# Channel-major products split over the two row halves of the matmul array

## What is computed

```
# first block
u = rmsnorm(x, norm_mix_g)
p = u @ w_in + b_in                                   # 1024 x 7424: q, kv, hq, hf, hi, hg, ga, gb
y_attn = sliding_window_sink_attention(aq, ak, av)    # 16 heads, window 128
y_hgrn = hgrn2_branch(hq, hf, hi, hg)                 # 8 heads, chunks of 64
merged = sigmoid(gate_a) * (y_attn @ w_branch_attn) + sigmoid(gate_b) * (y_hgrn @ w_branch_hgrn)
h = x + merged @ w_out
h = h + (silu(u2 @ w_ffn_gate) * (u2 @ w_ffn_up)) @ w_ffn_down
# second block
z, xbc, dt, q, k, v = split(h2 @ w_in_2)
x = x + g_m * (concat(ssd_mixer(z, xbc, dt), chunk_attention(q, k, v)) @ w_out_2)
x = x + g_f * ((silu(g) * val) @ w_down_2)            # g, val = causal_dwconv(h3 @ w_up_2)
```

## Time and profile before

| | |
|---|---|
| median of three runs | 795.62 us (795.6 to 796.41) |
| profiled execution, first to last instruction (span) | 794.3 us |
| what the median has beyond the span | 1.3 us |
| PE busy | 782.8 us, 99% |
| PE weight loads busy | 713.8 us, 90% |
| DVE busy | 598.9 us, 75% |
| ACT busy | 490.2 us, 62% |
| DMA | 161.1 MB, 203 GB/s on average |
| channel-major matmuls (L1799) | 3288 |

### The profile page before, as it was taken

The page is one execution under the profiler, slowest core; times in us unless marked ns, Lnnn a source line. Parts: engine busy times, 40 slices in busy tenths (PEclk is TensorE's granted clock), DMA queues, the critical chain, the costliest instruction groups (busy, mean ns, idle before and its releaser), DMA issues. The chain is left out here.

```text
span 794.3 us, 13466 instructions
## 1 busy us (share of the span) xinstructions
PE 782.8 (99%) x5534; PEld 713.8 (90%) x5534; DVE 598.9 (75%) x804; ACT 490.2 (62%) x746; POOL 17.9 (2%) x38
## 2 busy tenths in 40 slices
PE   8999999999999999999999999999999999999996
PEld 8999979999999888888888888999789999999885
DVE  5576786667876867787869897897968787777464
ACT  6778889567743565444434267966758767666441
POOL 3000001000200000000000000001000000000000
PEclk9999999999999999999999999999999999999999
DMA  8873544457444467799878993734362756555611
GB/s 303 295 240 134 191 130 158 160 169 256 160 159 160 158 214 257 233 308 310 283 277 299 359 364 122 258 112 157 107 212 87 256 164 206 165 166 180 238 54 54
DMA packets 105677, 161.10 MB, mean 203 GB/s; under 512 B 4480, under 2 KB 51856, under 8 KB 105616
## 3 DMA queue, kind: packets, MB, share of 16 engines
q1 hardware_dynamic: 105472, 159.97, 60.2%
q10 hardware_dynamic: 144, 0.26, 0.1%
HBM read 159.16 MB, written 1.06 MB: 202 GB/s over the span
## 5 line engine op out<-in xcount | busy, mean ns | idle before, releaser
L1127 DVE TENSOR_TENSOR wL<-raw,wH 128x2048 fp32r<-128x2048 f32 (+2 forms) x142 | 284.5, 2008 | 88.1 <-ACT wH L715 83.7
L1799 PE MATMUL ps<-p1H,wH 128*128 128x256 f32 x968 | 276.8, 287 | 1.8 <-DVE arena L1127 0.8
L1799 PE MATMUL ps<-p1H,wL 128*128 128x256 f32 x968 | 273.2, 283 | 0.0
L1799 PE MATMUL ps<-p1L,wH 128*128 128x256 f32 x968 | 271.8, 283 | 0.0
L715 ACT ACTIVATE wH<-raw 128x2048 fp32r<-128x2048 f32 (+1 forms) x114 | 211.9, 1863 | 85.4 <-PE ps L1802 43.6
L1799 PEld LDWEIGHTS ps<-p1H,wH 128*128 128x128 f32 x968 | 185.4, 192 | 6.4 <-issue 2.6
L1799 PEld LDWEIGHTS ps<-p1H,wL 128*128 128x128 f32 x968 | 185.5, 192 | 0.0
L1799 PEld LDWEIGHTS ps<-p1L,wH 128*128 128x128 f32 x968 | 184.8, 192 | 0.1
L1802 PE MATMUL ps<-wH,p1H 128*128 128x512 f32 (+1 forms) x236 | 91.1, 386 | 0.0
L1802 PE MATMUL ps<-wL,p1H 128*128 128x512 f32 (+1 forms) x236 | 90.2, 382 | 0.0
L1802 PE MATMUL ps<-wH,p1L 128*128 128x512 f32 (+1 forms) x236 | 90.1, 382 | 0.0
(11 more groups left out here) (306 smaller groups left out, 1018.4 us busy)
## 6 DMA issues: line engine op xcount, KB each, us to landing
raw<-in_w_in SPq DMA_DIRECT2D x37, 1024.0 KB, 5.1
raw<-in_w_ada SPq DMA_DIRECT2D x24, 1024.0 KB, 5.5
raw<-in_w_up SPq DMA_DIRECT2D x44, 512.0 KB, 4.8
raw<-in_w_ffn_gate SPq DMA_DIRECT2D x22, 512.0 KB, 4.5
raw<-in_w_ffn_up SPq DMA_DIRECT2D x22, 512.0 KB, 5.9
raw<-in_w_ffn_down SPq DMA_DIRECT2D x10, 1024.0 KB, 5.5
raw<-in_w_down SPq DMA_DIRECT2D x10, 1024.0 KB, 5.1
raw<-in_w_out SPq DMA_DIRECT2D x8, 1024.0 KB, 5.1
```

Of the source, the lines that this page charges most:

```text
L1127: return v.tensor_tensor(o, a, b, op)
L1799: last = mm(ps[:, t[1], 0:T], wt[:, slot, k, t[2]:t[2] + P], at_[:, k0 + k, :], start=st, stop=en)
```

## The change

Channel-major panels that came to the last branch of `panel` get one of their own. Each 128-row product is written as two products of 64 rows. A panel goes in four steps: tiles (0, 1), (2, 3), (1, 0), (3, 2). In a step, the first tile of the pair takes its lower 64 rows (partitions 0 to 63) of all four row blocks and the second its upper 64 rows, in turns, upper first; two steps later the halves are changed over, so that each tile has had both. The number of matmuls and of weight loads of such a panel doubles, to 96. Before each step PE waits until the step before the last has ended (`halves_written`), counted on a new semaphore `row_halves` or on `tile_done`. In a last part the tiles 0 and 1 end with the third step, 2 and 3 with the fourth. The operands, the accumulation in the banks and all other branches stay. To have a semaphore to spare, the ten of `hprep` that one engine each raises in a fixed order (on ACT hE1 to hE5, on DVE hdm, hQp, hKp, hdl, hKk) become two counters, `h_exp` and `h_mul`; the waits name the same events.

```diff
+H_EXP = {"mid": 1, "-mid": 2, "start": 3, "chunk": 4, "end": 5}
+H_MUL = {"mid": 1, "q": 2, "k": 3, "end": 4, "k_end": 5}
...
+        def h_exp(s, what):
+
+            return on.h_exp, 5 * s + H_EXP[what]
+
+        def h_mul(s, what):
+
+            return on.h_mul, 5 * s + H_MUL[what]
...
@@ the matmul engine, hA @@
-                    pe.wait_ge(on.hKp, s + 1)
-                    pe.wait_ge(on.hKk, s + 1)
+                    pe.wait_ge(*h_mul(s, "k_end"))
...
@@ the matmul engine, panel @@
+            halves_written, halved = [], [0]
+
             def panel(name, part):
                 q = PIDX[name, part]
                 g = GROUPS[name]
@@ -1850,6 +1855,35 @@
                                 last = product(t, k, only=(1,))
                         if name in NORM_OF and k < 2:
                             late_turn(NORM_OF[name], 6 + k)
+                elif [t[0] for t in g["tiles"]] == ["cm"] * 4:
+                    for step_, (low, high) in enumerate(((0, 1), (2, 3), (1, 0), (3, 2))):
+                        for written in halves_written[-2] if len(halves_written) > 1 else ():
+                            pe.wait_ge(*written)
+                        halves_written.append([])
+                        first_visit = part == 0 and step_ < 2
+                        for m in sorted((low, high)) if first_visit else ():
+                            if (name, m) in BANKFREE:
+                                pe.wait_ge(*BANKFREE[name, m])
+                        for k in range(nk):
+                            if step_ == 0 and name in FIRST_USE:
+                                pe.wait_ge(*operand_ready(name, k0 + k))
+                            for x, (wt, at_) in enumerate(((wH, aH), (wH, aL), (wL, aH))):
+                                for m, rs in ((high, slice(C, P)), (low, slice(0, C))):
+                                    _, bank, c = g["tiles"][m]
+                                    last = mm(ps[:, bank, 0:T], wt[rs, slot, k, c:c + P], at_[rs, k0 + k, :],
+                                              start=first_visit and k == 0 and x == 0,
+                                              stop=final and step_ > 1 and k == nk - 1 and x == 2)
+                                    if final and step_ > 1 and k == nk - 1 and x == 2:
+                                        last.then_inc(on.tile_done, 1)
+                                        halves_written[-1] = [(on.tile_done, TILE[name, m])]
+                                    elif k == nk - 1 and x == 2 and m == 3 and step_ == 3:
+                                        halves_written[-1].append(USED[q])
+                                    elif k == nk - 1 and x == 2:
+                                        last.then_inc(on.row_halves, 1)
+                                        halved[0] += 1
+                                        halves_written[-1] = [(on.row_halves, halved[0])]
+                        if (name, part, step_) == ("bc", 0, 1):
+                            dt_turn()
                 else:
                     for m, t in enumerate(g["tiles"]):
                         if part == 0 and (name, m) in BANKFREE:
```

More of the change, by code:

```diff
@@ L250, in build @@
         on.g_done = ctx.enter_context(nc.semaphore("g_done"))
[L251 to L258, removed]
+        on.h_exp = ctx.enter_context(nc.semaphore("h_exp"))
+        on.h_mul = ctx.enter_context(nc.semaphore("h_mul"))
         on.hQq = ctx.enter_context(nc.semaphore("hQq"))
@@ L264, in build @@
         on.hb_done = ctx.enter_context(nc.semaphore("hb_done"))
-        on.hdl = ctx.enter_context(nc.semaphore("hdl"))
-        on.hdm = ctx.enter_context(nc.semaphore("hdm"))
         on.hf_log = ctx.enter_context(nc.semaphore("hf_log"))
@@ L274, in build @@
         on.hs_done = ctx.enter_context(nc.semaphore("hs_done"))
+        on.row_halves = ctx.enter_context(nc.semaphore("row_halves"))
         on.hsh = ctx.enter_context(nc.semaphore("hsh"))
@@ L675, in _ @@
                 elif e[0] == "hprep" and e[2] == 2:
-                    pool.wait_ge(on.hE3, e[1] + 1)
-                    pool.wait_ge(on.hQp, e[1] + 1)
+                    pool.wait_ge(*h_exp(e[1], "start"))
+                    pool.wait_ge(*h_mul(e[1], "q"))
                     pool.tensor_tensor(hQ, hQ, T2, ALU.mult).then_inc(on.hQq, 1)
@@ L1043, in _ @@
                     if e[2] == 0:
-                        act.wait_ge(on.hdm, s + 1)
-                        nc.scalar.activation(T2, T1, ACT.Exp).then_inc(on.hE1, 1)
+                        act.wait_ge(*h_mul(s, "mid"))
+                        nc.scalar.activation(T2, T1, ACT.Exp).then_inc(on.h_exp, 1)
                     elif e[2] == 1:
-                        act.wait_ge(on.hE1, s + 1)
-                        nc.scalar.activation(T1, T1, ACT.Exp, scale=-1.0).then_inc(on.hE2, 1)
+                        act.wait_ge(*h_exp(s, "mid"))
+                        nc.scalar.activation(T1, T1, ACT.Exp, scale=-1.0).then_inc(on.h_exp, 1)
                     elif e[2] == 2:
-                        act.wait_ge(on.hQp, s + 1)
-                        nc.scalar.activation(T2, hB, ACT.Exp).then_inc(on.hE3, 1)
-                        nc.scalar.activation(E5[:], hB[:, :, C - 1:T:C], ACT.Exp).then_inc(on.hE5, 1)
-                    else:
-                        act.wait_ge(on.hdl, s + 1)
-                        nc.scalar.activation(T1, T1, ACT.Exp).then_inc(on.hE4, 1)
+                        act.wait_ge(*h_mul(s, "q"))
+                        nc.scalar.activation(T2, hB, ACT.Exp).then_inc(on.h_exp, 1)
+                        nc.scalar.activation(E5[:], hB[:, :, C - 1:T:C], ACT.Exp).then_inc(on.h_exp, 1)
+                    else:
+                        act.wait_ge(*h_mul(s, "end"))
+                        nc.scalar.activation(T1, T1, ACT.Exp).then_inc(on.h_exp, 1)
                         if s:
@@ L1558, in _ @@
                         dve.wait_ge(on.hk_done, 4 * s + 4)
-                        tt(f(T1), bc, bc[:, :, C // 2 - 1:C // 2].broadcast_to([P, 16, C]), ALU.subtract).then_inc(on.hdm, 1)
+                        tt(f(T1), bc, bc[:, :, C // 2 - 1:C // 2].broadcast_to([P, 16, C]), ALU.subtract).then_inc(on.h_mul, 1)
                     elif e[2] == 1:
@@ L1562, in _ @@
                             dve.wait_ge(on.scores_done, NU1)
[L1563 to L1566, removed]
+                        dve.wait_ge(*h_exp(s, "mid"))
+                        tt(hQp, hQ, T2, ALU.mult).then_inc(on.h_mul, 1)
+                        dve.wait_ge(*h_exp(s, "-mid"))
+                        tt(hKp, hK, T1, ALU.mult).then_inc(on.h_mul, 1)
                     elif e[2] == 2:
-                        dve.wait_ge(on.hKp, s + 1)
-                        tt(f(T1), bc[:, :, C - 1:C].broadcast_to([P, 16, C]), bc, ALU.subtract).then_inc(on.hdl, 1)
+                        dve.wait_ge(*h_mul(s, "k"))
+                        tt(f(T1), bc[:, :, C - 1:C].broadcast_to([P, 16, C]), bc, ALU.subtract).then_inc(on.h_mul, 1)
                     elif e[2] == 3:
-                        dve.wait_ge(on.hE4, s + 1)
-                        tt(hK, hK, T1, ALU.mult).then_inc(on.hKk, 1)
+                        dve.wait_ge(*h_exp(s, "end"))
+                        tt(hK, hK, T1, ALU.mult).then_inc(on.h_mul, 1)
                 elif k == "hA":
@@ L1583, in _ @@
                     bank = (7, 5, 6)
-                    dve.wait_ge(on.hE5, s + 1)
+                    dve.wait_ge(*h_exp(s, "chunk"))
                     dve.wait_ge(on.hkv_psum, 2 * s + 1)
```

## The result

The changed kernel takes 802.68 us (median of 4 runs, 802.36 to 802.89), the kernel before 795.88 beside it (795.6 to 796.41): a ratio of 1.0082, interval 1.0070 to 1.0093. The forecast was 781.2. The profiled execution spans 800.9 us, against 794.3: 6.6 us more, where 14.4 less were forecast.

What follows compares the result with a forecast made beforehand. PE was taken to bound the kernel; 22.3 us less for products, 5.9 more for changes of form and 2.0 more for tile ends and softmax gave 14.4 less: 781.2 us from 795.6, range 770 to 803 (0.9).

Steps and rivals of the forecast that it cites:

- The products: 2784 channel-major products on PE, each split into a pair of halves: pitch from 0.120 to 0.112 us, 22.3 us less.
- rows 5: Trace rows of hB before the change: 64-row products streaming 128 columns at the slow rate, 0.112 us a pair.
- rows 6: Trace rows before the change: full products that stream 128 columns, 0.110 us apiece.
- Loads of halves cost nothing more: In a pair on PE, the second half with its own weight load adds no time; by the skill's pricing, 259 us.
- Changes of form: PE switching between full rows and 64 rows or other forms: 31 more changes at 0.19 us, 5.9 us more.
- Waits between the halves of a panel: PE's wait before each of a panel's four steps for the step before the last: 0.
- Tiles that end later: Tiles ending in twos in last parts: 0.7 us more at k2, whose scores wait for ACT's copies; 0 elsewhere.
- Softmax beside the panels: Attention stretch, probabilities not ready at pt, units 0 and 1 with little room: 1.3 us more, including similar in hgrn and ssd.
- Semaphores: Ten semaphores merged into two counters, each wait naming the same event: 0.
- The bubble stays with each half: Rival: the 0.013 us gap belongs to every weight change, pair pitch stays 0.120; 802.5 us, chance 0.16.
- Two fast streams don't go together: Rival: a pair of halves costs what 512 columns do, 0.227 us; 1100 us in all, chance 0.08.
- The other two: Rivals: bubble goes altogether, pitch 0.109 to 0.110, 775.5 us, chance 0.13; tiles' ends hold it, 787 us, chance 0.06 (787 to 793).

Runs made afterwards that it cites:

- the last kernels: Kernel before, but both token operands stream past held high weights as one 512-column matmul: in u1 to u10 800.3 us, in six of these groups 794.99 us.
- the kernel of other forms: Changed kernel with u1 to u10 in pairs, single halves, quarters, single quarters or whole products, some matmuls left out; pitch 0.12 us, no comparable total.

## Why the prediction failed, step by step

*The products, 22.3 us less: the step that failed.* It said "I take 0.112, the pitch of the only half-array pairs with the same loads". Measured is 0.120 for 2784 pairs, so 0.0, the lower bound that I had named ("none of it goes, 0.120"). The pairs of rows 5 streamed 128 columns, where a whole product has 0.112 as well (the prediction had this from rows 6); they bounded the load and told nothing of what lies above it. The choice between the bounds went by the row that looked most like the new instructions (rows held, columns loaded), not by the row that shared what was in question (columns streamed at the fast rate, with its gap). The only such rows were the earlier trace rows, 0.120 and 0.227, which show the same 0.013 at both sizes: I had put this under "for it" and weighed it at 0.16.

*Loads of halves cost nothing more:* right. Two loads a pair pass in 0.12 us, and even four a set of quarters. The Trainium skill ("TensorE: Matmul & The Clock Gate", section LDWEIGHTS (loading the stationary operand)) is right of one load, 128 columns at an estimated 107 ns beside the floor of 111, and loads for different rows are not to be added up.

*Changes of form, 5.9 us:* right in kind and nearly in size. 0.19 was read at hB, and 0.177 is the mean of 20 in u. The first panel came 0.41 us earlier and the last 6.55 later. Of these 6.96, 2.3 are the waits at hf0, hi0 and k2; 4.6 remain, 0.15 for each of 31. Three places gave back 0.6 to 0.7 us each, which is part of why it is less than 31 x 0.177 = 5.5; smaller shifts of waits, either way, weren't added up. At z it was PE's wait of 0.7 for DVE in the kernel before (at L2104), which is gone. Behind each of the two hB the next panel's upper halves start while hB's last products, in the lower half alone, still go (timeline of PE, after; L2050 is hB):

```profile
155.57 0.61 PE L2050 MATMUL ps<-arena 64*128 64x128 f32 x4
155.91 0.38 PE L1873 MATMUL ps<-p1H,wH 64*128 64x256 f32 x1
156.01 0.38 PE L2050 MATMUL ps<-arena 64*128 64x128 f32 x2
156.13 0.28 PE L1873 MATMUL ps<-p1L,wH 64*128 64x256 f32 x1
```

From the start of hB to the next panel it is 1.98 us before and 1.35 after; some 0.2 of that are the changes of form that are gone, the rest is work that ran on idle rows. Halves do gain where rows are idle, as here.

*Waits between the halves of a panel, 0:* right, all 20 panels of u are as long as before.

*Tiles that end later:* the sum had 0.7 at k2, and 0.95 came. Elsewhere I wrote 0, with the reason that transposes, scores or `pt` lie between. At hq0 and hf0 that reason was wrong: nothing there waits for a bank, but the softmax of the next unit waits for ACT and DVE, which were held up, 0.86 and 0.53. I priced the last tile, and it was the first one that moved furthest, from a quarter to three quarters of the part.

*Softmax beside the panels, 1.3 us:* some 1.4 was lost, at unit 3, for which I had foreseen room of 0.5 to 1 us, and at unit 4, which I had left out for its token-major panel. At unit 1, where I saw no room, pt costs 0.31, its two changes of form and no wait. A right number with the wrong cause, by luck: it belongs to the tiles' ends.

*Semaphores, 0:* right, 0.9998.

*The rivals.* "The bubble stays with each half" gave 802.5 and 802.68 came, and its condition holds as written. That it hit within 0.2 us is luck: it had 5.9 for the changes of form and about 1 for waits, where some 4.6 and 2.3 came. "Two fast streams don't go together" is refuted by the pitch: a pair takes 0.120 and not 0.227. The other two need a pitch below 0.120 at 256 columns, which no form of the product showed. The range held the time, since it was drawn to reach this case.

*What stays open.* Whether the 13 ns belong to the change of weights or to each matmul can't be told here: every product in this kernel is preceded by its own load. The two matmuls of a product of the last kernels cost 0.236 + 0.117 where 0.227 + 0.120 was expected; whether the two pieces in which they are read or written make the difference wasn't tried.

## What to carry to other kernels

When the floor of a pitch is read from an instruction that resembles the new one, see first whether the quantity in dispute exists in that row: a row at the slow end of another limit (here the load, 0.111 to 0.112 us) hides it. Dividing a full product by rows gives nothing when all rows are held already; it costs 0.18 us for each change of form, and it moves the end of the first tiles, so ask who evacuates tile 0 and what stands behind it, not only who waits for the last. To lose part of the gap, hold the weights and stream more columns, and count who has to add up the result.

## What the runs showed of the hardware

A product of TensorE with a load of 128 columns has a pitch of 0.111 to 0.112 us with 8 or 16 columns streamed and with 128 to 240 at the fast rate, and 0.120 at 256. At 256 this holds for one half, two halves, four quarters and whole products, and for another bank each time.

The clock fell where mostly 32 rows were busy. In the kernel of other forms, windows over u4 and u5 (four quarters at once), over the start of u6 (one quarter), over the rest of u6 with u7 and the first 3 us of u8, and within u8 (whole); columns are the span, busy us of PE, PEld, DVE, ACT and POOL, the granted clock, DMA share and GB/s:

```profile
654.00:683.00 29.00, 26.13 (x728) 22.93 (x732) 18.88 (x25) 14.95 (x22) 0.00 (x0) 1.00 0.50 156
685.00:695.00 10.00, 9.26 (x70) 8.23 (x69) 6.76 (x11) 5.94 (x11) 0.00 (x0) 0.64 0.30 91
695.00:735.00 40.00, 37.88 (x207) 34.44 (x207) 12.92 (x17) 12.67 (x22) 0.00 (x0) 0.50 0.30 93
739.00:758.00 19.00, 18.49 (x149) 17.79 (x149) 12.54 (x15) 10.68 (x16) 0.00 (x0) 1.00 0.44 139
```

PE was over 90% busy by its records all the while, and one quarter alone passed at 0.12 us at first; then the granted clock went from 1.0 to 0.5 (2.4 to 1.2 GHz), the pitch to 0.21, and within u8 it was full again. PE stops for its own last product once in 12 products there, but in u4 and u5 as well, where the clock stayed at 1.0, so the stops alone don't explain it. With one half alone, in u2 and u3, the clock stayed at 1.0:

```profile
632.00:642.00 10.00, 10.00 (x101) 10.00 (x100) 7.71 (x12) 7.18 (x10) 0.00 (x0) 1.00 0.59 182
```

It is one observation in one kernel, and why it fell wasn't tried.
